# Cached keys of a paged decoder: from float32 products to three products of the rounded format

## What is computed

```python
latent = jnp.concatenate([past_latent, latent_new], axis=1)
k_nope = jnp.einsum('bsc,chd->bshd', latent, w_uk)
k = jnp.concatenate([k_nope, krope_of_all_heads], axis=-1)
k = _rmsnorm(k, g_qk_k)
k = jnp.concatenate([k[..., :QK_NOPE], _rope(k[..., QK_NOPE:], pos_k)], axis=-1)
s = jnp.einsum('bqhd,bkhd->bhqk', q, k) * scale
```

## Time and profile before

| | us |
|---|---|
| median of 3 runs | 1328.42 |
| lowest and highest run | 1321.75, 1332.19 |
| the profiled execution, its own time | 1320.99 |
| span of the profiled execution | 1319.3 |
| mean granted clock of TensorE | 0.974 |

### The profile page before, as it was taken

The page is one execution under the profiler, slowest core; times in us unless marked ns, Lnnn a source line. Parts: engine busy times, 40 slices in busy tenths (PEclk is TensorE's granted clock), DMA queues, the critical chain, the costliest instruction groups (busy, mean ns, idle before and its releaser), DMA issues.

```text
span 1319.3 us, 24253 instructions
## 1 busy us (share of the span) xinstructions
PE 1237.7 (94%) x9344; PEld 1103.1 (84%) x9344; DVE 816.2 (62%) x1392; ACT 509.3 (39%) x908; POOL 191.7 (15%) x337
## 2 busy tenths in 40 slices
PE   4998989988999899999999899899899998999998
PEld 4985767767989599999999677677699977999998
DVE  5566685767574577664556666757756556766442
ACT  4231322434343355553332324233443424655331
POOL 1234343320000000000012534224100000000000
PEclk8999999998999899999999899899899998999999
DMA  8624565571457845554565257557445784555552
GB/s 327 237 55 147 168 185 172 171 253 65 160 196 302 364 136 185 188 173 183 192 239 200 67 170 229 149 153 216 168 159 192 286 319 193 175 177 192 178 175 96
DMA packets 75090, 250.42 MB, mean 190 GB/s; under 512 B 11440, under 2 KB 44544, under 8 KB 54368
## 3 DMA queue, kind: packets, MB, share of 16 engines
q1 hardware_dynamic: 58896, 194.05, 41.8%
q0 software_dynamic: 13968, 47.57, 11.1%
q10 hardware_dynamic: 2112, 7.26, 1.4%
HBM read 241.60 MB, written 7.46 MB: 189 GB/s over the span
## 4 chain that ended last, share of the span: by engine, by line
PE 76%; DVE 9%; DMA 5%; issue 4%; ACT 3%; PEld 1%; POOLq 0%; POOL 0%; DVEq 0%; ACTq 0%; PEldq 0%
PE ps L1427 48%; PE ps L1436 18%; DMA ring<-in_units 3%; PE ps L1703 2%; DMA big<-in_pages 2%; DVE ring_r L745 2%; PE ps L1860 1%; PEld ps L1427 1%; DVE ssn L1071 1%; DVE xg_r L761 1%; DMA xT<-in_xt 1%; PE ps L1662 1%; PE ps L1663 1%; PE ps L1715 1%; ACT big_r L437 1%
## 5 line engine op out<-in xcount | busy, mean ns | idle before, releaser
L1436 PE MATMUL ps<-wuq_b,latT 128*128 128x260 f32 x1024 | 252.7, 396 | 13.7 <-ACT sc L437 11.7
L1427 PE MATMUL ps<-qkA_r,ring_r 128*128 128x264 f32 x880 | 252.7, 287 | 0.0
L1436 PEld LDWEIGHTS ps<-wuq_b,latT 128*128 128x128 f32 x1024 | 192.6, 194 | 59.0 <-issue 13.3
L365 POOL DMA_DIRECT2D big<-in_pages x256 | 138.7, 542 | 216.8 <-issue 200.9
L1427 PEld LDWEIGHTS ps<-qkA_r,ring_r 128*128 128x128 f32 x880 | 168.8, 192 | 0.0
L1427 PE MATMUL ps<-big_r,ring_r 128*128 128x264 f32 x512 | 145.5, 284 | 0.0
L745 DVE TENSOR_TENSOR ring_r<-ring,latT_r 128x2048 fp32r<-128x2048 f32 x42 | 96.2, 2292 | 60.4 <-ACT latT_r L437 59.5
L437 ACT ACTIVATE latT_r<-ring 128x2048 fp32r<-128x2048 f32 x42 | 80.4, 1915 | 108.3 <-DMA ring<-in_units 108.3
L437 ACT ACTIVATE qkA<-ps 128x512 f32<-128x512 f32 x86 | 51.0, 593 | 163.2 <-PE ps L1436 163.1
L1427 PE MATMUL ps<-xg_r,latT_r 128*128 128x264 f32 (+1 forms) x384 | 110.7, 288 | 0.0
L1427 PE MATMUL ps<-qkA_r,latT_r 128*128 128x264 f32 x320 | 94.5, 295 | 15.3 <-DVE xg_r L761 15.0
(11 more groups left out here) (370 smaller groups left out, 2945.8 us busy)
## 6 DMA issues: line engine op xcount, KB each, us to landing
ring<-in_units SPq DMA_DIRECT2D x136, 1024.0 KB, 4.9
big<-in_pages POOLq DMA_DIRECT2D x256, 144.0 KB, 3.4
latT<-in_pages SPq DMA_DIRECT2D x256, 128.0 KB, 2.7
big<-in_units SPq DMA_DIRECT2D x16, 1024.0 KB, 11.7
mat<-in_mats POOLq DMA_DIRECT2D x2, 2048.0 KB, 11.2
xg<-in_memt POOLq DMA_DIRECT2D x2, 1024.0 KB, 6.9
out_mk<-latT ACTq DMA_DIRECT2D x2, 1024.0 KB, 3.9
out_mv<-latT ACTq DMA_DIRECT2D x2, 1024.0 KB, 6.4
```

What stands on the lines that cost most here:

```text
L365: pool.dma_start(lat[:, s, pg, :], pages[bass.ds(at_page[pg] * DEPTH + l, 1), :, 256:544] .rearrange("a p n -> p (a n)")).then_inc(lat_in[ ...
L1427: ins = mm(out, a(i, k), b(j, k), start=first and k + n == 0, stop=last and k == KD - 1 and n == 2)
L1436: ins = mm(out, a, b, start=i == 0, stop=i == len(pairs) - 1)
```

## The change

The products of the cached keys are made of rounded parts. `wuq_b` becomes `wuq_r`, with a high and a low part of w_uk and of the query's columns; the query's 4 columns stand ahead of w_uk for even samples and behind it for odd ones, so that w_uk stands there once. The 16 places of `latT` are divided: 5 pairs for raw pages and 3 pairs for high parts; the low part overwrites the raw page. ScalarE makes the high part of the pair three ahead (`key_high`), behind its copy of the scores, VectorE the low part (`key_low`), behind its reduce; three pairs are split ahead of the first sequence. TensorE waits for the low part instead of the load, and makes 12 matmuls a pair. SP's loads go through the ring of five.

```diff
--- before.py
+++ after.py
@@ -79,11 +79,11 @@
 
 SIGNALS = dict(
 
-    tile_ready=0, unit_used=SLOTS, wide_used=0, pair_ready=8, mean_ready=0,
+    tile_ready=0, unit_used=SLOTS, wide_used=0, pair_ready=5, mean_ready=0,
 
     unit_hi=0, op_hi=0, x_sq=0, s_lat_sq=0, s_sq=0, lat_sq=0, qk_sq=0, gla_sq=0, mem_sq=0, km_sq=0, xq_sq=0,
     kr_sq=0, pair_sq=2, ff_hi=0, root=0, d_root=0,
-    gate_soft=0, gate_exp=0, soft_exp=0, dec_exp=0, x_exp=0, xs_exp=0,
+    key_hi=0, key_lo=0, gate_soft=0, gate_exp=0, soft_exp=0, dec_exp=0, x_exp=0, xs_exp=0,
 
     tile_free=4, unit_lo=0, op_lo=0, lat_used=2, pair_sc=2, pair_sum=3, moment=0, d_moment=0,
     x_new=1, x_part=8, sq_used=4, gain_in=0, ssum_ready=0, z_ready=0,
@@ -106,6 +106,18 @@
 def part_of(b, n, lag):
 
     return PARTS.get(b * 8 + n - lag)
+
+
+RAW, HIGH = 5, 3
+PAIRS = B * PAGES // 2
+
+
+def raw_of(q):
+    return slice(2 * (q % RAW), 2 * (q % RAW) + 2)
+
+
+def high_of(q):
+    return slice(2 * (RAW + q % HIGH), 2 * (RAW + q % HIGH) + 2)
 
 
 POOL_STEPS = 16
@@ -150,7 +162,7 @@
         gvs_n = sb("gvs_n", [B, 256])
         y = sb("y", [P, 4 * T])
         rBm = sb("rBm", [P, NM + 2])
-        wuq_b = sb("wuq_b", [P, 2, 2, 260])
+        _, wuq_r = twin("wuq", [P, 2, 2, 264])
         qt = sb("qt", [P, 2, B, H])
         qblk = sb("qblk", [P, B, 4, H])
         snew = sb("snew", [P, B, H])
@@ -267,7 +279,7 @@
         dve_step, act_step, pool_step = sem("dve_step"), sem("act_own"), sem("pool_step")
         unit_in = [sem(f"unit_in{s}") for s in range(SLOTS)]
         wide_in = [sem(f"wide_in{s}") for s in range(SLOTS)]
-        lt_in = [sem(f"lt_in{g}") for g in range(4)]
+        lt_in = [sem(f"lt_in{s}") for s in range(RAW)]
         lat_in = [sem(f"lat_in{s}") for s in range(2)]
         STORES = 7
         once_in, con_in, layer_in, mg_in = (sem(n) for n in ("once_in", "con_in", "layer_in", "mg_in"))
@@ -312,10 +324,11 @@
                 for b in range(B):
                     at_page = page_numbers(mybir.EngineType.SP, b * PAGES)
                     for pg in range(PAGES):
+                        q = l * PAIRS + (b * PAGES + pg) // 2
                         src = pages[bass.ds(at_page[pg] * DEPTH + l, 1), :, :].rearrange("a p n -> p (a n)")
                         if pg % 2 == 0:
                             sp.wait_ge(sems["pair_ready"], at["pair_ready"].free())
-                        sp.dma_start(latT[:, pg, :], src[:, 0:256]).then_inc(lt_in[pg // 4], 16)
+                        sp.dma_start(latT[:, raw_of(q).start + pg % 2, :], src[:, 0:256]).then_inc(lt_in[q % RAW], 16)
                 sp.wait_ge(sems["mix_heads"], l + 1)
                 sp.wait_ge(stored, 16 * (STORES * l + 5))
                 sp.sem_inc(passed["sp"], 1)
@@ -558,15 +571,24 @@
                         last.then_inc(sems["soft_exp"], 1)
 
 
+                def key_high(n):
+
+                    if n < PAIRS:
+                        q = l * PAIRS + n
+                        act.wait_ge(lt_in[q % RAW], 32 * (q // RAW + 1))
+                        f(latT_r[:, high_of(q), :], latT[:, raw_of(q), :], ACT.Copy).then_inc(sems["key_hi"], 1)
+
                 def keys(b, mem=False):
 
+                    sums, scores = (slice(4, 260), slice(0, 4)) if b % 2 == 0 else (slice(0, 256), slice(256, 260))
                     for pair in range(PAGES // 2):
                         act.wait_ge(sems["pair_ready"], at["pair_ready"].next())
                         act.wait_ge(sems["pair_sum"], at["pair_sum"].free())
                         q = pair % 2
-                        f(psq[(at["pair_sum"].n - 1) % 3].rearrange("p (g c) -> p g c", g=2), ps[:, 4 + 2 * q:6 + 2 * q, 0:256],
+                        f(psq[(at["pair_sum"].n - 1) % 3].rearrange("p (g c) -> p g c", g=2), ps[:, 4 + 2 * q:6 + 2 * q, sums],
                           ACT.Square).then_inc(sems["pair_sq"], 1)
-                        f(sc[:, b % 2, 2 * pair:2 * pair + 2, :], ps[:, 4 + 2 * q:6 + 2 * q, 256:260], ACT.Copy).then_inc(sems["pair_sc"], 1)
+                        f(sc[:, b % 2, 2 * pair:2 * pair + 2, :], ps[:, 4 + 2 * q:6 + 2 * q, scores], ACT.Copy).then_inc(sems["pair_sc"], 1)
+                        key_high(b * (PAGES // 2) + pair + HIGH)
                         if b and pair == 1:
                             d_power(of_decode, P, 64)
                         if b and pair == 2:
@@ -599,6 +621,8 @@
                     act.wait_ge(sems["dec_in"], at["dec_in"].next())
                     f(pr[:, :, 0:H], scw[:, :, :], ACT.Exp, scale=QK ** -0.5).then_inc(sems["dec_exp"], 1)
 
+                for n in range(HIGH):
+                    key_high(n)
                 for b in range(B):
                     keys(b, b == B - 1)
 
@@ -834,7 +858,9 @@
                 dve.wait_ge(con_in, 16)
                 def prepare(b):
 
-                    step(v.tensor_copy(wuq_b[:, b % 2, :, 256:260], qt[:, :, b, :]))
+                    c = 0 if b % 2 == 0 else 260
+                    step(v.tensor_copy(wuq_r[:, 0, :, c:c + 4], qt[:, :, b, :]))
+                    step(v.tensor_tensor(wuq_r[:, 1, :, c:c + 4], qt[:, :, b, :], wuq_r[:, 0, :, c:c + 4].bitcast(FP32), ALU.subtract))
                     tell("seq_in")
                     step(v.tensor_copy(qbs[:, b % 2, :], qblk[:, b, :, :].rearrange("p j h -> p (j h)")))
                     tell("rot_in")
@@ -862,8 +888,8 @@
                         tell("s_lat")
                     elif i == 9:
                         dve.wait_ge(layer_in, 64 * (l + 1))
-                        for s in range(2):
-                            step(v.tensor_copy(wuq_b[:, s, :, 0:256], w_uk))
+                        step(v.tensor_copy(wuq_r[:, 0, :, 4:260], w_uk))
+                        step(v.tensor_tensor(wuq_r[:, 1, :, 4:260], w_uk, wuq_r[:, 0, :, 4:260].bitcast(FP32), ALU.subtract))
                         step(v.tensor_copy(s_raw[NOPE:QK, 1, :].rearrange("p (h b) -> p h b", b=B),
                                            z[NOPE:QK, KR, TP:T].unsqueeze(1).broadcast_to([ROPE, H, B])))
                         t = tile()
@@ -1065,6 +1091,14 @@
                             tell("mix_heads")
 
 
+                def key_low(n):
+
+                    if n < PAIRS:
+                        q = l * PAIRS + n
+                        wait("key_hi")
+                        v.tensor_tensor(latT_r[:, raw_of(q), :], latT[:, raw_of(q), :], latT_r[:, high_of(q), :].bitcast(FP32),
+                                        ALU.subtract).then_inc(sems["key_lo"], 1)
+
                 def pair(s, n):
 
                     wait("pair_sq")
@@ -1124,6 +1158,7 @@
                     s, before = b % 2, b - 1
                     for n in range(PAGES // 2):
                         pair(s, n)
+                        key_low(b * (PAGES // 2) + n + HIGH)
                         fill(b, n)
                         if n == 0 and b:
                             scores(before)
@@ -1167,6 +1202,8 @@
                             split_unit(hi_mk)
 
                 last = B - 1
+                for n in range(HIGH):
+                    key_low(n)
                 for b in range(B):
                     if b == last:
                         dve.wait_ge(stored, 16 * (STORES * l + 5))
@@ -1466,7 +1503,7 @@
 
             pe.wait_ge(pool_step, 1)
             pe.sem_inc(sems["unit_used"], SLOTS)
-            pe.sem_inc(sems["pair_ready"], PAGES // 2)
+            pe.sem_inc(sems["pair_ready"], RAW)
             for l in range(DEPTH):
                 def sample(i):
 
@@ -1685,11 +1722,14 @@
                     q = n % 2
                     pe.wait_ge(sems["pair_sq"], at["pair_sq"].free())
                     pe.wait_ge(sems["pair_sc"], at["pair_sc"].free())
-                    if n % 2 == 0:
-                        pe.wait_ge(lt_in[n // 2], 64 * (l * B + b + 1))
-                    for pg in (2 * n, 2 * n + 1):
-                        ins = product(ps[:, 4 + 2 * q + pg % 2, 0:260],
-                                      [(latT[:, pg, P * c:P * c + P], wuq_b[:, b % 2, c, :]) for c in range(2)])
+                    wait("key_lo")
+                    at_pair = l * PAIRS + b * (PAGES // 2) + n
+                    w0 = 4 * (b % 2)
+                    for a in range(2):
+                        hi, lo = (latT_r[:, of(at_pair).start + a, :] for of in (high_of, raw_of))
+                        ins = product(ps[:, 4 + 2 * q + a, 0:260],
+                                      [(x[:, P * c:P * c + P], wuq_r[:, j, c, w0:w0 + 260]) for c in range(2)
+                                       for x, j in ((hi, 0), (hi, 1), (lo, 0))])
                     ins.then_inc(sems["pair_ready"], 1)
 
                 def values(b):
```

## The result

The changed kernel takes 1386.9 us (median of 4 runs, 1380.32 to 1392.79) against 1328.84 us for the kernel before on the same chip: 1.0443 times as long, with a 95% interval of 1.0379 to 1.0507. The forecast was 1.1% slower and its range ended at 1366. The direction was right; the loss is four times as large.

A forecast was written before the change was run, and what follows sets the result against it. VectorE was to replace TensorE as the key stages' bound: 204.0 and 200.8 us of work plus 22.6 idle a layer, 6.3 and 7.9 us longer; with 0.5 for w_uk's splits, 14.7 us slower, 1343 us, range 1312 to 1366.

The forecast's parts named there:

- TensorE's part: Key products on TensorE: 1.43 us a pair for 1.81, saving 0.38 us a pair, 49 us over 128 pairs.
- VectorE's part: Key stages: subtractions and prepare() add 41.4 us a layer, taking VectorE's occupation to 204.0 and 200.8 us.
- What VectorE must still wait for: VectorE's idle time left in each layer's key stage: 22.6 us; to break even, 16.3 and 14.7 us.
- the sign of being right: Key stages: VectorE's wait for ScalarE would fall from 52 us to near 20 a layer.
- (a): Start of the key stage: pair 0 waits for the first subtraction, until 85.2; VectorE idles 5 us a layer.
- (b): TensorE and VectorE tied at n=5 and n=6: 1.7 us idle in each of eight sequences, 13.6 us a layer.
- (c): Sequences 5 and 7, which have other waits: 2 us more idle each, 4 us a layer.
- What lies beside other work: ScalarE's copies and page loads through five pairs of buffer: don't bound, price 0; at most one landing more, 5.7 us.
- R1: Rival, faster: each sequence as long as its busier engine, plus the start's 5 us; 1308 to 1316 us; chance 0.20.
- R2: Rival, no change: VectorE's 405 us keeps TensorE's present overhead of 30 us; 1328, from 1316 to 1341; chance 0.33.
- R4: Rival, slower by the clock: TensorE's stalls in the key stages bring 1.2 GHz; 1355 to 1375 us; chance 0.14.
- R5: Rival: rounded products of keys run slower than those of the weights, 2.9 us a pair, 130 us more; chance 0.03.

The follow-up runs named there:

- e1: Changed kernel with VectorE's subtraction shrunk to 4 columns and the third product taking the high part again: 1327.63 us, ratio 1.0024 to the kernel before.
- e2: Kernel before, float32 products kept, with an unread VectorE reduce of 128x512 added after each pair's reduce: 1378.46 us, ratio 1.0411.
- e8: Kernel before with half of the cached keys' products left out: 1311.74 us, ratio 0.9888.
- e3: Changed kernel with unread products on TensorE at its waits, to keep it busy there: 1369.9 us, ratio 1.0374 to the kernel before.
- e4: Changed kernel with float32's fourth product, low x low, added back: 1377.78 us, ratio 1.0426 to the kernel before.
- e10: Kernel before with unread products on TensorE at five places of its stalls: 1314.41 us, ratio 0.9932.
- e14: Kernel before with an unread VectorE reduce added after the pair's own in pairs 0 to 3 of each sequence only: 1343.22 us, ratio 1.0145.
- e15: Kernel before with an unread VectorE reduce added after the pair's own in pairs 4 to 7 of each sequence only: 1345.58 us, ratio 1.0161.
- e5: Changed kernel with VectorE's subtraction moved to the loop body's end, ahead of the wait for the next squares: 1362.28 us, ratio 1.0272 to the kernel before.
- e12: Kernel before with half of the cached keys' products left out and unread products at TensorE's waits: 1313.16 us, ratio 0.992.

## Why the prediction was wrong

**TensorE's part: right.** Four pairs that nothing interrupts, from the windows of L1473:

```profile
301.70:308.00 6.30, 5.98 (x48) 5.80 (x48) 1.00 0.92 281
```

48 products in 5.98 us are 1.50 us a pair, for 1.43 forecast and 1.81 before: 0.31 us saved a pair where 0.38 was counted. But the saving bought nothing: e1 keeps it, loses VectorE's subtraction, and stands at 1.0024. The busy time of the two stages did not even fall (406.3 us for 406.2), since the clock in them fell from 0.97 and 0.96 to 0.88 and 0.86, and that took back what the shorter products saved.

**VectorE's part: right.** 201.1 and 197.7 us of occupation for 204.0 and 200.8. The mean of the subtraction is 721 ns, where L1157 has 680; 128 x 0.041 = 5 us in all. The trace has them where the prediction put them: in sequence 0, beside GpSimd's operations of 1.5 to 1.9 us, three subtractions of layer 0 took 1.53, 1.30 and 1.95 us and three of layer 1 took 1.13, 1.30 and 1.96; all others took 0.68.

**"What VectorE must still wait for": the step that failed.** It gave 5 + 13.6 + 4 = 22.6 us a layer; the trace has 40.6 and 46.3. Of that, VectorE's wait for ScalarE is 36.0 and 41.6 us, where some 20 were given as the sign of being right. (a), the start, held: pair 0 at 84.5, forecast 85.2, and 7.3 us of waits in sequence 0 for 5 + 1.7. (b), the 13.6 us, is the term that failed. It took the 1.7 us that VectorE waited in sequence 3, where it was already the bound, as what every sequence keeps. In layer 0 sequences 3 and 6 did fall to 0.9 us each, but 1, 2 and 4 kept about 7.8, 7.3 and 5.2 us of the 9.3, 8.1 and 8.1 they had, although 5.2 us of work were added in each; in layer 1 they kept 9.0, 5.6 and 4.0. (b) treats idle time as a store which added work draws on one for one. The runs show that it isn't: e2 adds nothing but VectorE work, its idle time falls only to 38.1 us, and each microsecond costs 0.70. Put ahead of the wait, the same instruction costs 0.27. The account that fits both, and the two places of the timeline above, is this: VectorE idles in its wait for squares, and an instruction behind the reduce does not stand in that gap; it pushes `exponents`, `kr_scaled` and the freed tiles later, TensorE meets them at n=5 and n=6, and the next squares come later in turn. The cost by place is measured; the steps between are read from the timeline. (c) named sequences 5 and 7 as the exceptions, with 2 us more each. They kept 8.4 and 5.2 us in layer 0, where they grew by only 0.5 each, and 14.0 and 6.5 in layer 1, where sequence 5 grew by 6.0. The sequences given as unchanged or shorter, 1, 2 and 4, grew by 4.6, 3.0 and 3.5. That TensorE had been busy all the time there was read as room that its saving would open. It was not: e8 takes 116 us of its work and gains 14.9.

**What lies beside other work: right.** ScalarE's copy waited 0.9 us for loads in the whole execution; the ring of five is enough, and e1 has copies and ring and no loss.

**The rivals.** R1 and R2 fell with the same assumption, R1 by more. R4 called the clock under 0.9 in the stages, and it is 0.88 and 0.86, with 79 us of TensorE's idle time for about 90; but as the main cause it fell. It expected the clock to lengthen the sequences past VectorE's need. e3 brings the clock to 0.962 and recovers 0.7% of 4.4%, and e4, at a clock of 0.960 to 0.961 in all its runs, still loses 4.3%. A smaller share of the clock isn't excluded. The Trainium skill's "TensorE: Matmul & The Clock Gate", section on HAM oscillation, has idle gaps bring the half clock back; the traces here agree (sequence 4 went from 1.00 with no idle time to 0.89 with stalls), and what giving it back was worth is 0.7% in e10 and, not clear of its interval, in e3. R5: no.

What stays open: which single wait weighs most, and what the low clock adds to it. e14 and e15 say that both halves of a sequence carry it. Moving `values` or the product of the rotary keys a pair later on TensorE, or letting GpSimd make the low part, was not tried.

## What to carry to other kernels

A busy share of 93% does not name the bound when engines that work in order wait for each other in turn: take work away from the engine, or add some, and read the slope. Here 78 us less of TensorE's busy time (e8) gave 15, and 32 us more of it in the changed kernel (e4) cost nothing. The Trainium skill's "Perfetto Trace Analysis", Identifying the Most-Contended Engine, says to optimise the engine with the highest occupancy first, and to judge TensorE's headroom by MFU (the matmul work done as a share of what the engine could do in the time) and the busy share of its weight loads rather than by its matmuls' busy time. By the weight loads TensorE stands at 303.87 / 435.8 = 70% of the two stages, beside VectorE's 67%: the lead of 93% over 67% is nearly gone, and these runs fit that better. When work must be added to an engine that waits once in each turn of a loop, put it ahead of the wait and not behind the step that others wait for (0.27 against 0.70 for each us; e5 got 1.7% back in this way), and price idle time by an inserted dummy instruction before it is counted as free.

## What the runs showed of the hardware that was not expected

- TensorE's busy time is no fixed cost: with 116 us of products less, its clock in the stages went from 0.97 and 0.96 to 0.88 and 0.83, and the busy time fell by 78.
- 35 unread products a layer, placed at stalls, took 0.7% off the kernel before (e10), with the mean clock at 0.984 for 0.974. In e12, 79 a layer left the clock of the stages where it was (0.88 and 0.87) and took nothing off e8's time.
- VectorE waits 4.6 us for GpSimd's first maximum over partitions in each layer's stage, though the instruction itself takes 0.39 us. The timeline of sequence 1, and the queue's own instruction of that line (count, ns, first and last start):

```profile
136.29 0.39 POOL L428 PARTITION_ALL_REDUCE mx<-mxp  x1 [20.79 <-issue]
```

```profile
L428 POOLq MODIFY_POOL_CONFIG  x4: 11/11/11, 130.6 to 806.1; - x4
```

The first and the last of these stand at 130.6 and 806.1 us, and the maxima that follow them start at 136.29 and 811.75: 5.7 us each. The Trainium skill's "GPSIMD Engine Reference", section Instruction dispatch, has this as the load of new code into the engine, some 6 us that no instruction of the profile shows, to be paid at the first call; the trace agrees with the size. It was there before the change as well: VectorE waited 5.3 us, and the two instructions started at 121.9 and 127.63 us. Whether it can be moved away from VectorE's chain, by a first call ahead of the stage, was not tried.
